# From the first layer's experts to the odd layer's first projection: sums, LN and first chunk in two token halves

## The reference

```python
x = LN(alpha * x + mixer(x))
x = LN(alpha * x + MoE(x))        # y = gate0 * expert0(x) + gate1 * expert1(x)
p = x @ w_in_odd                  # 1024 x 4608: q, k, v of three head groups
...
```

## Time and profile before

| | |
|---|---|
| median of 3 runs | 1220.41 us (1219.21 to 1221.7) |
| the profiled execution | 1221.2 us, its span 1219.4 us |
| TensorE matmul busy | 996.8 us (82%) |
| VectorE busy | 494.0 us (41%) |
| ScalarE busy | 286.1 us (23%) |
| mean DMA rate | 234 GB/s |

### The profile page before, as it was taken

The page is one execution under the profiler, slowest core; times in us unless marked ns, Lnnn a source line. Parts: engine busy times, 40 slices in busy tenths (PEclk is TensorE's granted clock), DMA queues, the critical chain, the costliest instruction groups (busy, mean ns, idle before and its releaser), DMA issues.

```text
span 1219.4 us, 14221 instructions
## 1 busy us (share of the span) xinstructions
PE 996.8 (82%) x5434; PEld 661.7 (54%) x5434; DVE 494.0 (41%) x1223; ACT 286.1 (23%) x495; POOL 107.5 (9%) x159
## 2 busy tenths in 40 slices
PE   6999999998288888785099999999983888787750
PEld 5878888886134323332078888888871333233320
DVE  3862575546523212111944343425555232111118
ACT  3444223132011212111032333323321122121110
POOL 4000000000112111111000000000002111111110
PEclk8989999999599989998589999999996999899995
DMA  8245332255979999993433222221495899999933
GB/s 232 70 69 104 69 70 69 90 221 218 403 318 423 424 423 424 425 423 148 161 104 103 70 70 70 81 90 39 166 372 218 334 424 424 424 425 425 422 147 150
DMA packets 73076, 284.81 MB, mean 234 GB/s; under 512 B 10860, under 2 KB 27260, under 8 KB 47408
## 3 DMA queue, kind: packets, MB, share of 16 engines
q1 hardware_dynamic: 57216, 232.80, 50.6%
q10 hardware_dynamic: 5184, 33.56, 6.6%
q0 software_dynamic: 10608, 17.54, 3.9%
HBM read 280.71 MB, written 23.07 MB: 249 GB/s over the span
## 4 chain that ended last, share of the span: by engine, by line
PE 60%; DMA 14%; SPq 11%; DVE 9%; issue 3%; ACT 2%; ACTq 0%; POOLq 0%; DVEq 0%; POOL 0%
PE bank L1861 16%; PE bank L1579 15%; DMA wgu<-in_w_up 11%; PE bank L1781 9%; SPq L411 6%; SPq L416 4%; PE bank L1803 4%; PE bank L1896 2%; PE bank L1597 2%; DVE h L1340 2%; PE bank L1929 1%; PE bank L1770 1%; PE bank L1683 1%; PE bank L1668 1%; PE bank L1606 1%
## 5 line engine op out<-in xcount | busy, mean ns | idle before, releaser
L1781 PE MATMUL bank<-wgu,xgt 128*64 128x512 f32 x1024 | 236.1, 614 | 31.7 <-DMA wgu<-in_w_up 28.2
L1781 PEld LDWEIGHTS bank<-wgu,xgt 128*64 128x64 f32 x1024 | 86.1, 142 | 177.7 <-issue 162.7
L1803 PE MATMUL bank<-wd,htt 128*64 128x512 f32 x512 | 116.9, 597 | 49.9 <-issue 49.9
L924 DVE TENSOR_TENSOR wl<-raw,wh 128x2048 fp32r<-128x2048 f32 x40 | 91.6, 2291 | 154.1 <-ACT wh L640 154.1
L640 ACT ACTIVATE wh<-raw 128x2048 fp32r<-128x2048 f32 x40 | 76.5, 1913 | 162.6 <-PE bank L1579 106.9
L1306 DVE TENSOR_TENSOR hh<-sg,bank 128x256 f32<-128x256 f32 x32 | 13.5, 421 | 235.4 <-ACT sg L791 235.4
L1803 PEld LDWEIGHTS bank<-wd,htt 128*64 128x64 f32 x512 | 40.4, 136 | 104.3 <-issue 104.3
L1861 PE MATMUL bank<-xt_hi,wh 128*128 128x512 f32 x192 | 76.4, 398 | 2.2 <-DVE wl L924 2.2
L1311 DVE COPY yt<-bank 128x512 f32<-128x512 f32 x32 | 22.1, 692 | 135.1 <-PE bank L1803 135.1
L1861 PE MATMUL bank<-xt_lo,wh 128*128 128x512 f32 x192 | 75.5, 393 | 0.0
L1861 PE MATMUL bank<-xt_hi,wl 128*128 128x512 f32 x192 | 75.5, 393 | 0.0
(11 more groups left out here) (320 smaller groups left out, 1566.6 us busy)
## 6 DMA issues: line engine op xcount, KB each, us to landing
wgu<-in_w_gate SPq DMA_DIRECT2D x64, 1024.0 KB, 24.3
wgu<-in_w_up SPq DMA_DIRECT2D x64, 1024.0 KB, 27.8
wd<-in_w_down SPq DMA_DIRECT2D x36, 1024.0 KB, 25.3
wd<-in_w_down ACTq DMA_DIRECT2D x28, 1024.0 KB, 11.7
raw<-in_w_in_even SPq DMA_DIRECT2D x16, 1024.0 KB, 7.6
raw<-in_w_in_odd SPq DMA_DIRECT2D x32, 512.0 KB, 4.4
y<-y_rows SPq DMA_DIRECT2D x8, 1024.0 KB, 7.9
h<-in_x SPq DMA_DIRECT2D x8, 512.0 KB, 5.0
```

What stands on the lines that cost most here:

```text
L924: dve.tensor_tensor(wl[slot][:, :, :], raw[slot][:, :, :], wh[slot][:, :, :], ALU.subtract)\
L1781: ins = pe.matmul(bank[2][B * b:B * (b + 1), :], xgt[:, k, B * b:B * (b + 1)], wgu[s][:, b, :, k, :], start=(k == 0), stop=(k == KT - 1))
L1803: ins = pe.matmul(bank[5 + n][B * b:B * (b + 1), :], htt[:, k, B * b:B * (b + 1)], wd[s][:, b, k, n * 512:(n + 1) * 512], start=(k == 0), ...
```

## The change

VectorE adds the experts' sums only for the left 512 columns. The right 512 are added by TensorE in PSUM: two matmuls with the gates on a diagonal (`dga`) and one with the identity, in banks 4 to 7. Statistics of the right half are read from PSUM. Tokens go in two halves (tiles 0 and 1, tiles 2 and 3): scales for two tiles, then VectorE normalises the left columns and ScalarE the right ones, without gain and bias. TensorE transposes 16 blocks, ScalarE applies gain and bias by feature (`lnx`) on the way to `xt_t`, and VectorE splits from there. The first chunk is multiplied for each token half, 256 columns a matmul, in the order unit 20 half 0, second turn, unit 21 half 0, unit 20 half 1, unit 21 half 1. Units 20 and 21 are loaded into buffers of their own (`early`) once 14 pairs' `down` are done and are split right after the experts. `h` itself gets gain and bias at `m` = 4. `keep_warm` is now 8. All units of the odd layer are read with feature rows p*8+k in place of k*128+p.

```diff
+        early_z = Zone(z.at, 16 * KB)
+        early = [early_z.take(f"early{i}", [P, 4, C], f32) for i in range(2)]
+        xt_t = Zone(z.at, 16 * KB).take("xt_t", [P, KT, T], f32)
...
+        dga = Zone(z.at, 4 * KB).take("dga", [P, NT, 2, P], f32)
...
-        def wait_ln(eng, n, t):
-            assert n % 2
-            eng.wait_ge(ln_out[t % 2], 2 * (n // 2) + t // 2 + 1)
+        def raw_of(u, slot):
+            return early[slot] if u in (U_ODD, U_ODD + 1) else raw[slot]
+        def turned(half, k):
+            b = ((4, 5, 2, 3), (6, 7, 4, 5))[half][k // 2]
+            return bank[b][:, k % 2 * 256:(k % 2 + 1) * 256]
+        def wait_ln(eng, t):
+            eng.wait_ge(ln_out[t % 2], t // 2 + 1)
...
+            def odd_unit(m):
+                (g, o), dst = ODD[m // 2], raw_of(U_ODD + m, m % 2)
+                w = xo.rearrange("(p k) c -> p k c", k=KT)[:, 4 * (m % 2):4 * (m % 2) + 4, :]
+                if o is None:
+                    sp.dma_start(dst[:, :, :], w[:, :, 2 * C:3 * C]).then_inc(raw_in[m % 2], 16)
+                    return
+                src = w.rearrange("p k (g s o c) -> p k g s o c", g=3, s=3, o=2)
+                for i in range(2):
+                    part = src[:, :, i + 1, 2, o, :] if g is None else src[:, :, g, i, o, :]
...
                         load_pair(l, (NFIX + j) % 3, e, TRIP * it + (NFIX + j))
+                if l == 0:
+                    sp.wait_ge(dn_done[0], TRIP * iters + (NFIX - 2))
+                    for m in range(2):
...
-            for m in range(18):
-                (g, o), u = ODD[m // 2], U_ODD + m
-                sp.wait_ge(w_lo, u + 1)
-                w = xo[m % 2 * 4 * P:(m % 2 + 1) * 4 * P, :]
-                if o is None:
-                    src = w[:, 2 * C:3 * C].rearrange("(k p) c -> p k c", p=P)
-                    sp.dma_start(raw[m % 2][:, :, :], src).then_inc(raw_in[m % 2], 16)
-                    continue
-                src = w.rearrange("(k p) (g s o c) -> p k g s o c", p=P, g=3, s=3, o=2)
-                for i in range(2):
-                    part = src[:, :, i + 1, 2, o, :] if g is None else src[:, :, g, i, o, :]
-                    sp.dma_start(raw[m % 2][:, :, 256 * i:256 * (i + 1)], part).then_inc(raw_in[m % 2], 16)
+            for m in range(2, 18):
+                sp.wait_ge(w_lo, U_ODD + m + 1)
...
                     pool.dma_start(lnt[:, l, i, :], w[l, 0:1, :].rearrange("a (p k) -> p (a k)", p=P)).then_inc(lnt_in, 16)
+            for i, w in enumerate((ln_g, ln_b)):
...
-            for t in (2, 3):
-                wait_ln(pool, 1, t)
...
                 act.wait_ge(unit_done, u + 1)
-                act.activation(wh[slot][:, :, :], raw[slot][:, :, :], ACT.Copy).then_inc(w_hi, 1)
...
+            def turned_half(half):
+                act.wait_ge(ls_ready, half + 1)
+                for t in (2 * half, 2 * half + 1):
+                    act.activation(h[:, t, C:D], bank[4 + t][:, :], ACT.Identity, scale=rstd[:, t:t + 1],
+                                   bias=nmr[:, 8 + t:9 + t]).then_inc(n_act, 1)
+                for k in range(KT):
+                    act.wait_ge(xt_tr, KT // 2 * half + k // 2 + 1)
+                    act.activation(xt_t[:, k, 256 * half:256 * (half + 1)], turned(half, k), ACT.Identity,
+                                   scale=lnx[:, 0, k:k + 1], bias=lnx[:, 1, k:k + 1]).then_inc(xt_a, 1)
             router(0)
             experts(0)
             for u in range(2):
-                split_xt(16, range(4 * u, 4 * u + 4))
                 split_unit(U_ODD + u, u)
+            act.wait_ge(lnx_in, 32)
+            act.wait_ge(w_lo, U_ODD + 4)
+            for half in range(2):
+                turned_half(half)
...
-                dve.tensor_tensor(wl[slot][:, :, :], raw[slot][:, :, :], wh[slot][:, :, :], ALU.subtract)\
+                dve.tensor_tensor(wl[slot][:, :, :], raw_of(u, slot)[:, :, :], wh[slot][:, :, :], ALU.subtract)\
...
+            def gate_diagonals():
+                for t in range(NT):
+                    for c in range(2):
+                        ins = dve.tensor_scalar(dga[:, t, c, :], ident[:, :], ga[:, c, t:t + 1], None, ALU.mult)
+                ins.then_inc(ga_diag, 1)
+            def add_left(t):
+                hs = h[:, t, 0:C]
+                dve.wait_ge(y2_in[t], 16)
+                for c in range(2):
+                    link(dve.scalar_tensor_tensor(hs, y2[t][:, c * D:c * D + C], ga[:, c, t:t + 1], hs, ALU.mult, ALU.add))
+                tile_stats(t, 0)
+                dve.wait_ge(right_ready, t + 1)
+                return dve.bn_stats(stat[:, 2 * t + 1, :], bank[4 + t][:, :])
+            def scales_and_left(half):
+                at = 2 * half
+                for t in (at, at + 1):
+                    ins = dve.bn_aggr(mv[:, t, :], stat[:, 2 * t:2 * t + 2, :])
+                link(ins)
+                rsqrt(mv[:, at:at + 2, 1], 2, at)
+                dve.scalar_tensor_tensor(nmr[:, 8 + at:10 + at], mv[:, at:at + 2, 0], -1.0, rstd[:, at:at + 2],
+                                         ALU.mult, ALU.mult).then_inc(ls_ready, 1)
+                dve.wait_ge(ls_ready, half + 1)
+                for t in (at, at + 1):
+                    dve.tensor_scalar(h[:, t, 0:C], h[:, t, 0:C], rstd[:, t:t + 1], nmr[:, 8 + t:9 + t],
+                                      ALU.mult, ALU.add).then_inc(n_dve, 1)
+            def split_turned(half, ks):
+                cols = slice(256 * half, 256 * (half + 1))
+                for k in ks:
+                    dve.wait_ge(xt_a, KT * half + k + 2)
+                    link(dve.tensor_copy(xt_hi[:, k:k + 2, cols], xt_t[:, k:k + 2, cols]))
+                    dve.tensor_tensor(xt_lo[:, k:k + 2, cols], xt_t[:, k:k + 2, cols], xt_hi[:, k:k + 2, cols],
+                                      ALU.subtract).then_inc(xt_l, 1)
+            def turn_and_split():
+                dve.wait_ge(h_scaled, 1)
+                add_left(0)
+                link(add_left(1))
+                scales_and_left(0)
+                add_left(2)
+                split_turned(0, (0, 2))
+                link(add_left(3))
+                split_turned(0, (4, 6))
+                scales_and_left(1)
+                split_turned(1, (0, 2, 4, 6))
+            def gain_and_bias():
+                dve.wait_ge(xt_tr, KT)
+                dve.wait_ge(ln_in, 2 * 32)
+                for t in range(NT):
+                    link(dve.tensor_tensor(h[:, t, :], h[:, t, :], lngb[:, 0, :], ALU.mult))
+                    link(dve.tensor_tensor(h[:, t, :], h[:, t, :], lngb[:, 1, :], ALU.add))
             for t in range(NT):
                 dve.wait_ge(x_in[t], 32)
             out_norm(0)
             route(0)
             experts(0)
-            add_experts(0)
-            layer_norm(1)
+            gate_diagonals()
             for u in range(2):
-                split_xt(16, range(4 * u, 4 * u + 4))
                 split_unit(U_ODD + u, u)
+            turn_and_split()
...
+                if m == 4:
+                    gain_and_bias()
...
-            for t in (2, 3):
-                wait_ln(pe, 1, t)
+            def right_halves():
+                pe.wait_ge(ga_diag, 1)
+                pe.wait_ge(h_scaled, 1)
+                for t in range(NT):
+                    pe.wait_ge(y2_in[t], 16)
+                    for c in range(2):
+                        pe.matmul(bank[4 + t][:, :], dga[:, t, c, :], y2[t][:, c * D + C:(c + 1) * D],
+                                  start=(c == 0), stop=False)
+                    pe.matmul(bank[4 + t][:, :], ident[:, :], h[:, t, C:D], start=False, stop=True).then_inc(right_ready, 1)
+            def turn_half(half):
+                pe.wait_ge(n_act, 2 * half + 2)
+                pe.wait_ge(n_dve, 2 * half + 2)
+                if half:
+                    pe.wait_ge(xt_a, 4)
+                for k in range(KT):
+                    for j in range(2):
+                        ins = pe.transpose(turned(half, k)[:, j * P:(j + 1) * P], h[:, 2 * half + j, k:D:KT], ident[:, :])
+                    if k % 2:
+                        ins.then_inc(xt_tr, 1)
+            def first_part(v, half):
+                if half == 0:
+                    pe.wait_ge(w_lo, U_ODD + v + 3)
+                pe.wait_ge(xt_l, 2 * KT + 4 * half + 2 * (v + 1))
+                cols = slice(256 * half, 256 * (half + 1))
+                for i in range(4):
+                    if v == 0 and half == 0 and i == 2:
+                        pe.wait_ge(xt_a, KT)
+                    for kk in range(4):
+                        k = 4 * v + kk
+                        for n, (xp, wp) in enumerate(((xt_hi, wh), (xt_hi, wl), (xt_lo, wh))):
+                            ins = pe.matmul(bank[i][:, cols], wp[v][:, kk, i * P:(i + 1) * P], xp[:, k, cols],
+                                            start=(k == 0 and n == 0), stop=(k == 7 and n == 2))
+                    if half and v and i < 3:
```

(34 more changed lines are left out.)

5 lines of the change are left out of this document (added).

## The result

The changed kernel takes **1206.29 us** (median of four, 1205.77 to 1210.09), the kernel before, run beside it, 1220.92 (four). The ratio is 0.988 [0.9863, 0.9897]: 14.6 us gained, where 10.8 were forecast. The profiled execution took 1206.5 us, its span 1204.7; that of before, 1221.2 and 1219.4.

What follows compares the result with a forecast made beforehand. Bound: TensorE's hole between layers, 6.3 us of transposes in 46.8 us while VectorE works. Chunk 0 ends at 626.5 + 1.3 + 0.6 + 0.5 = 628.9 against 639.7, 10.8 us earlier: 1209.6 us, range 1206.5 to 1217.

Steps and rivals of the forecast that it cites:

- The seam's mechanism: Between the layers, moe_done to unit 22: TensorE shares sums, tokens go in halves; chunk 0 ends near 629, not 639.7.
- The step of 256 columns: First odd chunk: each of 192 matmuls takes 0.121 us, between bounds of 0.114 and 0.228.
- Both rivals of the step: First odd chunk: weight load as floor, 0.19 a step, 1219.0 us, 6%; full price, 0.228 a step, 1225.5 us, 6%.
- The warming: TensorE behind moe_done: eight warming matmuls end at 584.0, and the right halves wait for them, not for the y tile.
- Gain and bias: VectorE at m = 4: eight whole-tile operations, 9.5 us, fit into 14.7 before unit 26 and cost nothing.
- Unit 22: Behind chunk 0: VectorE must split its weights, set scales and keep bank 0 first, costing 0.6 us.
- The rival of 2%: Seam: right halves come no sooner than VectorE would have made them, so VectorE would wait at every tile; 2%.
- moe_done stays at 574.4: End of the first layer's experts: time unchanged, since nothing ahead of it is taken away.
- the 0.8 us to the median: Whole kernel: the profiled execution lies 0.8 above the median of 1220.41, so 1210.4 becomes 1209.6.
- The cold restart: TensorE idle before the first odd matmul and second turn: clock falls cost 0 to 3.4 us, taken as 1.3.
- The gather's 0.5 us: Last gather of rows before moe_done: early weight loads delay it by 0 to 3.6 us, taken as 0.5.
- The rival of early loads and two cold restarts: Last gather and seam: 3.6 us instead of 0.5, and 3.4 instead of 1.3; gain 5.6, 1214.8 us, 16%.

## Why the prediction was right or wrong

Steps of the seam, in us from the issue of the y tiles (574.40 in the forecast, 570.64 after):

| step | forecast | after |
|---|---|---|
| right halves begin | 9.6 | 9.2 |
| first statistics of a right half done | 12.9 | 12.6 |
| scales of tiles 0 and 1 | 18.2 | 18.1 |
| first turn begins | 19.9 | 19.7 |
| first odd matmul | 24.2 | 24.1 |
| second turn begins | 32.7 | 33.1 |
| chunk 0 ends, unit 22 begins | 54.0 (54.5 with the gather) | 53.1 |

**Right.** The seam's mechanism: every step lies within 1 us of the forecast, in the order forecast. The step of 256 columns was put at 0.121 us between bounds of 0.114 and 0.228, and measured 0.12. Both rivals of the step are refuted by it, and a load of 0.19 is no floor. In a window of the first part 26 loads fill 3.00 us, 0.115 each, beside matmuls that fill it too:

```profile
599.00:602.00 3.00, 3.00 (x28) 3.00 (x26) 2.62 (x14) 0.00 (x0) 0.00 (x0) 1.00 0.00 0
```

The warming was named as what the right halves wait for, and the run without it confirms that. Gain and bias took 10.1 us and cost nothing. Unit 22 waits 0.64, where 0.6 was put. The rival of 2% was half right: VectorE waited at one tile only, but as the run without right halves on TensorE shows, behind eight warming matmuls they bring the second turn no sooner.

**The step that failed** is the first: "moe_done stays at 574.4: nothing ahead of it is taken away." Nothing was, and yet it came at 570.5 in the profiled execution. The kernel before had been profiled in an execution whose clock was at half from 66.9 to 73.7 us, in work that the change leaves alone. I took that as fixed, together with the 0.8 us to the median. The changed kernel's median of four lies in the lower cluster, and its profiled execution had no fall. The forecast for a profiled execution, 1210.4 us, is a time of the upper cluster (1209.99 to 1210.82). In the table the excess over 10.8 is 3.84 from the head and 1.35 from the seam, less 1.28 in the other stages, which is within their spread. With a fall in both profiled executions, the kernel without gain and bias took 11.05 us less than before, close to the 10.8. The range held no term for the draw; as the profiled execution had the fall, 3.8 us towards faster belonged in it. That the time missed the range by only 0.2 us is a matter of how many of four executions fell in the lower cluster: the median of six more was 1208.08, inside it.

**Terms that were mis-sized.** The cold restart was put at 1.3 us and cost nothing. The clock did fall, from 595.5 to 598.9, behind the 2.40 us of idle time ahead of 594.78; but as the prediction's bound of zero says, in the first part it is hidden by the wait for the second turn, where TensorE was idle for 1.51 us more. It didn't fall again in the seam:

```profile
594.00:598.00 4.00, 3.22 (x18) 3.25 (x19) 3.86 (x7) 0.82 (x2) 0.00 (x0) 0.69 0.01 4
...
602.00:606.00 4.00, 2.49 (x22) 2.29 (x21) 1.61 (x5) 2.94 (x6) 1.17 (x4) 1.00 0.00 0
```

The gather's 0.5 us was nothing: 18.73 us from the start of the last gate_up to moe_done, before and after. Together these 1.8 us, less 0.4 at the second turn, make up the 1.35 (0.5 of which, the gather's, the forecast had ahead of the seam). The rival of early loads and two cold restarts is thus refuted in both of its prices.

**Rules weighed.** The Trainium skill (TensorE: Matmul & The Clock Gate, Part 3, "The mechanism") says that a load overlaps a matmul in flight only with another row group, though the same section also has loads pulled ahead into a background weight buffer. The trace disagrees with the first for 256 columns too: with loads and matmuls one after the other, 0.115 us of load would leave nothing of a 0.12 us step. Its rule that transposes don't count for the clock gate (Part 4) was not put to the test in the changed kernel, whose second turn ran at full clock throughout. The kernel before with early weights disagrees with it once more: the granted clock rose at 614.1 when TensorE had run nothing but transposes since 608.58.

**Left open.** Why the clock falls in or behind `m_rows` in one execution and not in another, whether the change makes that rarer, and what the two groups of before are. All four profiled executions of the kernel before and its variants had a fall there, but all four were long ones of their kernel (2.8 to 7.2 us above its shortest), so they don't tell how often it comes.

## What to carry to other kernels

Ahead of a forecast, mark what in the one profiled execution may be a draw (a stretch at half clock inside busy work, with no idle time ahead of it), and put its whole price into the range on the side that it didn't draw. When one engine's serial work opens a hole, cut the tokens so that the other engine multiplies the first part while the second is prepared; that was worth more here (7.9 us, some 3 of them clock) than the earlier weights (3.9). Warm TensorE only until the data is there, and put whatever releases the next turn ahead of whatever is needed only later: these two small edits gave another 6.2 us of seam, a part of which may be the clock. Before giving idle TensorE a share of another engine's work, ask whether it can start as early: here, behind eight warming matmuls, it only kept the clock up.

## What the runs showed of the hardware

- An fp32r matmul of 256 columns takes half the time of one of 512: 0.12 us a step against 0.228, though each has its own weight load.
- The granted clock fell to half while TensorE was continuously busy, in or within 1.5 us behind a stretch of matmuls over 4 of 128 rows, and stayed there for 6.8 us, in some executions for 3.4. Whether it fell differed between executions with the same work there (six of ten profiled). Ten executions of the changed kernel form two clusters some 4 us apart.
- Sixteen transposes take 2.06 us at full clock and 3.68 at half, so where idle time ahead of a turn lets the clock fall (4.12 us of it did in the kernel without right halves on TensorE, 1.51 in the changed kernel didn't), it costs 1.6 us for the turn alone.
